# Hyena mixer: every second block of modulation rows is multiplied by GpSimd and summed by ScalarE

## The reference, cut to what matters

```python
sh1, sc1, g1, sh2, sc2, g2 = jnp.split((s_lat @ ada_w[i] + ada_b[i])[:, None, :], 6, axis=-1)
hx = x * (1 + sc1) + sh1
...
u = short_conv_centred(h @ w_in, conv_w, conv_b)          # 3 taps along the tokens
x1, x2, v = jnp.split(u, 3, axis=-1)
zz = x1 * fft_long_conv(v, hf[:, 0], fbias[0])
zz = x2 * fft_long_conv(zz, hf[:, 1], fbias[1])
y_lat = zz @ w_out
...
x = layer_norm(DEEPNORM_ALPHA * x + g1 * y_lat, ln_g[i, 0], ln_b[i, 0])
x = layer_norm(DEEPNORM_ALPHA * x + g2 * peer_ffn(x * (1 + sc2) + sh2, *peer_w), ln_g[i, 1], ln_b[i, 1])
```

## Time and profile before

| | us |
|---|---|
| median of 3 runs | 1860.39 (1859.46 to 1860.76) |
| the profiled execution | 1858.19 |
| its span | 1856.4 |
| TensorE busy | 1659.2 (89% of the span) |
| VectorE busy | 1446.8 (78%) |
| GpSimd busy | 540.4 (29%) |
| DMA of expert rows on the chain that ended last | 23% and 4% of the span |

### The profile page before, as it was taken

The page is one execution under the profiler, slowest core; times in us unless marked ns, Lnnn a source line. Parts: engine busy times, 40 slices in busy tenths (PEclk is TensorE's granted clock), DMA queues, the critical chain, the costliest instruction groups (busy, mean ns, idle before and its releaser), DMA issues.

```text
span 1856.4 us, 18264 instructions
## 1 busy us (share of the span) xinstructions
PE 1659.2 (89%) x5432; PEld 909.8 (49%) x5432; DVE 1446.8 (78%) x3491; ACT 595.5 (32%) x1483; POOL 540.4 (29%) x543
## 2 busy tenths in 40 slices
PE   8999999999989987989898999989999978787776
PEld 3787588544544433334343777545544423233332
DVE  6777895877678778988887799877787788777755
ACT  4564854232222223333322221122222323222222
POOL 0343000034333333333343000133333434333332
PEclk9999999999999999999999999989999999999999
DMA  8341239899999999999999685699999999999996
GB/s 355 144 143 46 114 145 370 338 364 426 427 423 427 426 426 426 391 426 426 416 423 425 244 317 222 246 414 424 427 426 427 426 428 425 425 426 424 422 427 258
DMA packets 96423, 664.34 MB, mean 358 GB/s; under 512 B 11421, under 2 KB 13438, under 8 KB 17476
## 3 DMA queue, kind: packets, MB, share of 16 engines
q0 software_dynamic: 74304, 536.90, 69.1%
q1 hardware_dynamic: 22020, 126.27, 17.7%
HBM read 662.02 MB, written 1.11 MB: 357 GB/s over the span
## 4 chain that ended last, share of the span: by engine, by line
PE 36%; DMA 27%; DVE 18%; issue 4%; ACT 1%; PEld 1%; PEldq 0%; DVEq 0%; POOL 0%; another core or an unknown queue 0%; POOLq 0%; ACTq 0%
DMA expert_rows<-in_p_uv,chosen_experts 23%; PE bank L1199 19%; DVE dot_products L2592 6%; DMA expert_rows_spare<-in_p_uv,chosen_experts 4%; PE bank L1155 3%; PE bank L980 3%; PE bank L1057 3%; DVE silu_c_row_and_products L1935 2%; PE bank L1414 1%; ACT weight_diagonal L1758 1%; PE bank L995 1%; DMA expert_rows<-in_p_uv,half_row_indices 1%; PE bank L1096 1%; PEld bank L1199 1%; PE bank L1122 1%
## 5 line engine op out<-in xcount | busy, mean ns | idle before, releaser
L1199 PE MATMUL bank<-expert_rows,weight_diagonal 128*128 128x512 f32 x1816 | 855.2, 613 | 140.1 <-ACT weight_diagonal L1758 138.5
L2592 DVE SCALAR_TENSOR_TENSOR dot_products<-expert_rows,bank 128x1024 f32<-128x1024 f32 x454 | 554.2, 1221 | 199.1 <-DMA expert_rows<-in_p_uv,chosen_experts 185.5
L1199 PEld LDWEIGHTS bank<-expert_rows,weight_diagonal 128*128 128x128 f32 x1816 | 338.4, 194 | 593.5 <-issue 351.3
L1465 POOL DMA_INDIRECT expert_rows<-in_p_uv,chosen_experts x450 | 424.7, 944 | 694.4 <-PE bank L1199 649.0
L1758 ACT ACTIVATE weight_diagonal<-constants,expert_weights 128x128 f32<-128x128 f32 x512 | 178.0, 394 | 239.2 <-DVE expert_weights L2520 234.7
L1750 ACT ACTIVATE expert_gelu<-expert_dots 128x2 f32<-128x2 f32 x260 | 52.7, 203 | 599.8 <-DVE dot_products L2592 599.5
L1465 POOL DMA_INDIRECT expert_rows_spare<-in_p_uv,chosen_experts x58 | 54.6, 942 | 470.7 <-DVE chosen_experts L2505 375.0
L1199 PE MATMUL bank<-expert_rows_spare,weight_diagonal 128*128 128x512 f32 x232 | 114.0, 615 | 22.3 <-ACT weight_diagonal L1758 22.3
L1474 POOL TENSOR_TENSOR weights_lo<-weight_block,weights_hi 128x1024 fp32r<-128x1024 f32 x22 | 53.2, 2418 | 120.7 <-ACT weights_hi L1521 120.7
L2592 DVE SCALAR_TENSOR_TENSOR dot_products<-expert_rows_spare,bank 128x1024 f32<-128x1024 f32 x58 | 70.8, 1221 | 22.2 <-DMA expert_rows_spare<-in_p_uv,chosen_experts 20.5
L1199 PEld LDWEIGHTS bank<-expert_rows_spare,weight_diagonal 128*128 128x128 f32 x232 | 43.3, 195 | 76.8 <-issue 43.1
(11 more groups left out here) (345 smaller groups left out, 2081.5 us busy)
## 6 DMA issues: line engine op xcount, KB each, us to landing
weight_block<-in_ada_rows SPq DMA_DIRECT2D x22, 1024.0 KB, 7.0
weight_block<-in_m_in_blocks SPq DMA_DIRECT2D x20, 1024.0 KB, 6.5
hyena_weight_block<-in_ada_rows SPq DMA_DIRECT2D x15, 1024.0 KB, 6.7
hyena_weight_block<-in_h_in_blocks SPq DMA_DIRECT2D x12, 1024.0 KB, 6.9
weight_block<-in_wq_blocks SPq DMA_DIRECT2D x11, 1024.0 KB, 7.4
expert_rows<-in_p_uv,chosen_experts POOLq DMA_INDIRECT x450
out_weights<-in_m_out_blocks SPq DMA_DIRECT2D x6, 1024.0 KB, 8.3
weight_block<-in_ada_shift SPq DMA_DIRECT2D x4, 1024.0 KB, 11.4
```

What stands on the lines that cost most here:

```text
L1199: last = mm(ps[b][:, :], dg[n % DIAG][:, :], uv[slot][:, D + h * 512:D + (h + 1) * 512], start=(r == 0 and k == 0), stop=end)
L1465: pool.indirect_dma_start(uv[slot][:, :], None, A[f"p_uv{l}"], bass.IndirectOffsetOnAxis(ap=chosen[:, s_, k:k + 1], axis=0)).then_inc(uv_l ...
L2592: stt(prod[:, :], uv[slot][:, 0:D], 1.0, rows_t, ALU.mult, ALU.mult, accum_out=dots[:, s_, k + j:k + j + 1]).then_inc(sem("dots_done"), 1)
```

## The change

GpSimd multiplies each of the blocks 9, 11, 13, 15, 17, 19, 21 and 23 by the row of SiLU(c) in place, in two tensor_tensor of 128x1024. ScalarE then takes the sum over each product with an Identity activation that has an accumulator (`row_sums`), at eight places of its list. VectorE keeps the dots of the other blocks, and its two bias steps of the gate and of the expert stage's shift and scale come later. SyncE's list of loads keeps its order, but a load that waited for VectorE's dots of one of the eight blocks now waits for ScalarE's sums. One dot of block 22 takes the place of the one of block 23 that stood in the expert stage's head.

```diff
-LAST_DOTS = 1
-HYENA_DOTS = (2, 2, 2, 2, 5, 3, 3, 3, 3, 3, 0, 0)
+HYENA_DOTS = (2, 0, 2, 0, 2, 2, 2, 2, 2, 0, 0, 0)
+SHARED_ROWS = (9, 11, 13, 15, 17, 19, 21, 23)
...
+    def shared_sums(b):
+
+        return 2 * sum(r < b for r in SHARED_ROWS)
     def stage_ada(l, b0, b1, ring=weight_ring):
 
         for b in range(b0, b1):
+            if l and b in SHARED_ROWS:
+                place[f"ada{l}_rows", b] = ring.add(rows(f"ada_rows{l}", b), (sem("shared_row_sums"), shared_sums(b + 1)))
+                continue
             ada_dots[0] += 2
...
         phase_end(pool, 1)
+        for h in range(2):
+            wait_read(pool, ("c_row", 0, h))
+        for b in SHARED_ROWS:
+            rows_ = block_in(pool, place["ada1_rows", b])
+            for half_ in range(2):
+                part = rows_[:, half_ * D:(half_ + 1) * D]
+                pool.tensor_tensor(part, part, c_rows[0], ALU.mult).then_inc(sem("shared_row_products"), 1)
         wait_full(pool, ("hout", 3))
...
-        for i in range(5):
+        def row_sums(b):
+
+            rows_ = block_in(act, place["ada1_rows", b])
+            for half_ in range(2):
+                m = 2 * b + half_
+                part = rows_[:, half_ * D:(half_ + 1) * D]
+                act.wait_ge(sem("shared_row_products"), shared_sums(b) + half_ + 1)
+                f(part, part, ACT.Identity, accum_out=ada[1][:, m // KD, m % KD:m % KD + 1]).then_inc(sem("shared_row_sums"), 1)
+
+        for i in range(3):
+            hyena_block(i)
+        row_sums(9)
+        for i in (3, 4):
             hyena_block(i)
         signal_tokens(0, 0)
-        for i in (5, 6):
-            hyena_block(i)
+        hyena_block(5)
+        row_sums(11)
+        hyena_block(6)
         signal_tokens(0, 1)
-        for i in (7, 8):
-            hyena_block(i)
+        row_sums(13)
+        hyena_block(7)
+        row_sums(15)
+        hyena_block(8)
         gate_copy(1, 0)
+        row_sums(17)
         hyena_block(9)
         signal_tokens(1, 0)
+        row_sums(19)
         hyena_block(10)
         signal_tokens(1, 1)
+        row_sums(21)
         hyena_block(11)
+        row_sums(23)
...
+            if l and part >= 2:
+                dve.wait_ge(sem("shared_row_sums"), shared_sums((part + 1) * KD // 2))
...
-        dots1 = [2 * KD]
+        dots1 = [m for m in range(2 * KD, 2 * HELD_ROWS) if m // 2 not in SHARED_ROWS]
...
-            if i == 4:
-                modulation_bias(1, 2)
-                gate_diagonal(1, 0)
         spectrum_products(0, 0)
         hyena_block(6)
+        modulation_bias(1, 2)
+        gate_diagonal(1, 0)
         spectrum_products(0, 1)
...
         hyena_block(9)
+        hyena_block(10)
         for part in (3, 4):
             modulation_bias(1, part)
         fold_gain(1, 1)
-        hyena_block(10)
         spectrum_products(1, 0)
...
-        for m in range(2 * HELD_ROWS, ADA_TILES - LAST_DOTS):
-            modulation_dot(1, m)
+        modulation_dot(1, 2 * HELD_ROWS)
```

More of the change, by code:

```diff
@@ L2404, in peer @@
             else:
-                for m in range(ADA_TILES - LAST_DOTS, ADA_TILES):
-                    modulation_dot(1, m)
+                modulation_dot(1, 2 * HELD_ROWS + 1)
                 modulation_bias(1, 5)
@@ L2669, in hyena_block @@
             for _ in range(HYENA_DOTS[i]):
-                modulation_dot(1, dots1[0])
-                dots1[0] += 1
+                modulation_dot(1, dots1.pop(0))
         def fold_signal(o, h):
```

## The result

The changed kernel takes 1881.23 us (median of 5 runs, 1878.94 to 1883.46) against 1860.39 (5 runs, 1859.46 to 1863.06): 20.8 us more, ratio 1.0117, 95% interval 1.0106 to 1.0128. The forecast was 1880, the range 1866 to 1887.

What follows compares the result with a forecast made beforehand. TensorE was taken to bound the Hyena stage, VectorE close behind, gathers the second expert stage. Delays accumulated as +3.4, +9.2, +16.5, +20.2 us; added to the 1860.39 median: 1880.6, stated as 1880, range 1866 to 1887.

Steps and rivals of the forecast that it cites:

- Step 1: Hyena stage, first spectrum product: block 14's load waits for block 11's sums; TensorE 3.4 us late after its last transform.
- Step 2: Up to order gate (0, 0): products of blocks 17 and 19 delay VectorE; inverse (0, 1) 9.2 us late so far.
- Step 3: Order gate (0, 1): block 20's load waits for block 17's sums behind the gate's copy; TensorE 16.5 us late so far.
- Step 4: Products of block 21 meet order gate (0, 1), of block 23 spectrum (1, 0); last inverse 20.2 us late so far.
- Step 5: From last inverse to first gather: TensorE works without a wait, `h_w_out` is in time, gather comes 20.2 us later.
- the ladder: The forecast's path through the Hyena stage: TensorE's durations kept, each start moved to its latest releaser; 20.2 us later.
- Only the queue: Rival: GpSimd and VectorE don't exclude each other, only late loads behind ScalarE's sums cost; 1867.5 us, chance 0.16.
- Only the lock: Rival: loads come early enough, only GpSimd's products holding up VectorE cost; +14 us, 1874.5 us, chance 0.09.
- Faster: Rival: VectorE's lighter list shows and TensorE's three waits for it (3.0 us) go; 1857.4 us, chance 0.06.
- the lock: VectorE instructions with two SBUF inputs and GpSimd's products exclude each other for whole instructions; 0 to 2.4 us per product.

Runs made afterwards that it cites:

- experiment 1: Complete change without GpSimd's 16 products; ScalarE sums the unmultiplied rows and loads still wait for those sums: 1866.04 us, ratio 1.0037 to the kernel before.
- experiment 4: Complete change with ScalarE's sums of block 17 moved ahead of the gate's copy: 1874.26 us, ratio 1.0074 to the kernel before.
- experiment 2: Complete change without ScalarE's 16 sums; GpSimd's products stay and loads wait for them instead: 1872.92 us, ratio 1.0070 to the kernel before.
- experiment 3: Complete change without ScalarE's sums and with each GpSimd product cut from 1024 columns to 8: 1852.93 us, ratio 0.9963 to the kernel before.
- experiment 6: Complete change, but GpSimd multiplies by a constant (one SBUF input) instead of the row of c: 1866.50 us, ratio 1.0040 to the kernel before.
- block 9 alone: Only block 9 shared, the other 14 dots back on VectorE in new places: 1857.65 us, again 1855.76; ratios 0.9986 and 0.9984 to the kernel before.
- quarters: Complete change with each GpSimd product cut into four pieces of 256 columns: 1868.23 us, ratio 1.0048 to the kernel before.
- no block shared: Kernel before with only the places of VectorE's dots, bias and diagonal changed, nothing shared: 1858.32 us, ratio 0.9996 to the kernel before.
- experiment 9: Only blocks 9 and 17 shared, products in four pieces, block 17's sums early, other dots respread: 1854.18 us, ratio 0.9971 to the kernel before.
- experiment 10: Complete change with products in four pieces and block 17's sums ahead of the gate's copy: 1864.52 us, ratio 1.0029 to the kernel before.

## Why the prediction was right, and where only its sum was

**Step 1**, first product after block 14's load. Forecast: sums of block 11 done at 1086.1, dots at 1090.8, spectrum at 1093.3. Measured, less 1.53: 1085.9, 1090.6, 1093.1. Step 7 was to start 3.4 late and is 4.2 late (1103.4 against 1099.20): TensorE's wait of 3.17 is as foreseen, the rest is the slower transform behind it (3.27).

**Step 2**, order gate (0, 0). Forecast 9.2 late, measured 6.1 (it begins at 1125.52). The product of block 17 took turns with one dot (3.17) and with the small bias instruction (2.19, which I had put at its bare time), not with two dots: 4.0 instead of 4.6. The main error is the product of block 19. I had it fall between the dots of block 18; it came behind both and fell into the gate itself, whose additions took 2.06 and 2.57 where they take 0.42. VectorE's four instructions and GpSimd's products of block 19:

```profile
1107.31 3.17 DVE L1968 SCALAR_TENSOR_TENSOR silu_c_row_and_products<-hyena_weight_block,silu_c_row_and_products 128x1024 f32<-128x1024 f32 x1
1110.52 2.19 DVE L1978 SCALAR_TENSOR_TENSOR modulation_columns<-modulation_columns,channel_vectors 128x8 f32<-128x8 f32 x1
...
1126.49 2.06 DVE L2754 TENSOR_TENSOR layer_norm_tmp<-layer_norm_tmp 128x256 f32<-128x256 f32 x1
1128.47 2.57 DVE L2755 TENSOR_TENSOR layer_norm_tmp<-layer_norm_tmp 128x256 f32<-128x256 f32 x1
```

```profile
1125.92 4.84 POOL L1490 TENSOR_TENSOR hyena_weight_block<-hyena_weight_block,silu_c_row_and_products 128x1024 f32<-128x1024 f32 x2 [13.22 <-DMA hyena_weight_block<-in_ada_rows]
```

So TensorE's wait split into 3.47 and 2.62. Step 9 begins at 1136.5 (1138.06 less 1.53), 1.0 later than the 1135.5 of the forecast.

**Step 3**, block 20. Sums done 1139.5 (measured 1139.3), landed 1144.2 (1144.1), order gate (0, 1) at 1146.7 (1146.6), step 10 16.5 late (16.9). Experiments 1 and 4 show this wait by leaving out the products and by moving the line.

**Step 4**, last inverse: 20.2 late forecast, 22.2 measured, of which 2.3 are the slower step 10: VectorE waits 3.71 us for its copy (at 1163.57) before it can go on to this inverse's product.

**Step 5** was wrong in its sum: "from there TensorE works without a wait" holds, but the last inverse ran at 0.69 of the clock and gave another 1.6. The transposes come 23.9 late, the gather 23.8.

**The sum.** The forecast of 20.2 counted only waits. In the traces it was 15.8 us of waits and 8.1 of slower matmuls, 23.9 together. So the place and kind of each cause were right, the waits were put 4 us too long, and a term of twice that size, the clock behind each wait, was not in the ladder at all. The row for it stood in the profile before: inverse (0, 1) took 5.44 us in the earlier trace rows behind a wait, inverse (1, 1) 3.84 with 0.56 ahead of it. The two errors offset each other by half and left the forecast 3.7 us short of the traces. That it meets the medians (20.2 against 20.8) is luck beyond that: the medians lie 4.5 us closer together than the two traces.

**Terms.** A product took 2.4 to 2.6 us (4.73 to 5.18 for a pair, 6.66 where they took turns with VectorE), as said (16 of 2.40 are 38.4, not the 38.6 of the forecast); a pair of sums 2.1 to 2.2 instead of 2.4; the load 4.8 from issue to landing instead of 4.7.

**Rivals.** *Only the queue* was to give 1867.5; experiment 1, in which only it is left, gives 1866.0. *Only the lock*: 1874.5; experiment 2 gives 1872.9. Both were sized rightly and neither is the whole. *Faster* was priced at 3.0 us; experiment 3 shows that the relief is worth 6.4 where nothing stands against it. One reason is again the clock: 2.4 us of the stage are matmuls that run faster when the waits are gone.

**The price of the lock.** The Trainium skill, GPSIMD Engine Reference, section 8 (Key points), names contention with VectorE instructions that have two SBUF inputs and gives no price. In this case the price is what is left of the GpSimd instruction that is met: 1.95 to 2.2 us in ten meetings of the complete change, 0.5, 1.1 and 1.6 in three; VectorE's instructions with a bank input keep their 0.68 and 0.87.

## What to carry to other kernels

Work moved to GpSimd is not moved to an idle engine if it has two SBUF inputs and VectorE works on SBUF beside it: look at which VectorE instructions it will meet, cut it into short pieces, and put it where VectorE waits. A ring buffer whose release moves to another engine takes over that engine's place in the order: ask what stands ahead of the releasing instruction. And a wait of TensorE can cost more than its length: look for a row of the same matmuls behind a wait and one without, and count the difference into the range.

## What the runs showed of the hardware beyond that

- A GpSimd tensor_scalar of 128x1024 with one SBUF input is slower than the product with two (2.94 us against 2.4 to 2.6) and yet delays VectorE by only 0.6 to 0.8 us each (experiment 6).
- The small bias instruction of VectorE (128x8) was held up by 2 us beside a product: an instruction's size is no protection.
- A cut has a price: a pair of products takes 4.9 us whole (block 9 alone) and 5.96 in eight pieces.
- The same 32 matmuls of an inverse took 3.73 us at clock 1.00 and 5.44 at 0.69; step 10's took 7.07 at 1.00 and 9.38 at 0.75.
- Not every wait of TensorE is followed by slower matmuls, and the extra doesn't grow with the wait. The last inverse took 3.84 us behind waits of 1.70 (quarters) and 1.71 (no block shared), and 5.47 behind 1.82 (experiment 9), 2.67 (experiment 10) and 3.60. Step 10 took 7.07 us behind a wait of 1.95 in experiment 4 and 8.76 behind one of 1.95 in experiment 2.
